# Scores of attentions A, B and C over all 128 rows with zeros for the other head; one visit of TensorE per attention slot; B's two maps combined before they are transposed

## The reference, cut to what matters

```
A: 8 query heads, 2 key heads, width 64, window |i-j| <= 128, a sink logit in the denominator
C: 3 patterns of 8 heads, width 64 (C0: window 64; C1, C2: among tokens of one residue mod 4)
D: 8 heads, width 96, all 512 keys
B (differential), 4 heads, two maps of width 64 each, all 512 keys, values of width 128:
    sc = einsum('bqmhd,bsmhd->bmhqs', q, k) * scale - slope[h] * |pos_q - pos_s|
    a  = softmax(sc, axis=-1)
    a  = a[:, 0] - lam[h] * a[:, 1]
    o  = einsum('bhqs,bshv->bqhv', a, v);   o = rms_norm(o, subln_g) * (1 - lam_init)
```

## Time and profile before

| | |
|---|---|
| time, median of 3 | 3000.47 us (3000.18 to 3017.97) |
| the profiled execution | 3004.72 us, its span 3002.9 us |
| PE busy | 2820.7 us, 94% of the span |
| PE weight load | 2267.0 us, 75% |
| DVE busy | 1566.0 us, 52% |
| ACT busy | 1179.0 us, 39% |
| chain that ended last | PE 81%, DVE 9%, ACT 4%, issue 4% |
| mean granted TensorE clock | 0.978 |
| DMA | 217.62 MB, mean 72 GB/s |

### The profile page before, as it was taken

The page is one execution under the profiler, slowest core; times in us unless marked ns, Lnnn a source line. Parts: engine busy times, 40 slices in busy tenths (PEclk is TensorE's granted clock), DMA queues, the critical chain, the costliest instruction groups (busy, mean ns, idle before and its releaser), DMA issues.

```text
span 3002.9 us, 44753 instructions
## 1 busy us (share of the span) xinstructions
PE 2820.7 (94%) x13358; PEld 2267.0 (75%) x13358; DVE 1566.0 (52%) x3238; ACT 1179.0 (39%) x2387; POOL 0.6 (0%) x5
## 2 busy tenths in 40 slices
PE   5999989989989998999979999898899899999998
PEld 4889978666667887888868898776666678788887
DVE  5454476444445445555644544764354454465655
ACT  4444444434433234332434444534444332342432
POOL 0000000000000000000000000000000000000000
PEclk9999999889999999999989999999999999999999
DMA  4212222001112332333332122220111123223332
GB/s 152 72 48 72 78 63 85 12 29 41 45 37 78 94 96 78 99 98 99 99 100 64 44 78 79 67 85 1 36 43 50 31 91 98 92 85 98 95 96 91
DMA packets 141819, 217.62 MB, mean 72 GB/s; under 512 B 14777, under 2 KB 69387, under 8 KB 141195
## 3 DMA queue, kind: packets, MB, share of 16 engines
q1 hardware_dynamic: 132521, 200.62, 21.4%
q10 hardware_dynamic: 9058, 14.06, 1.4%
HBM read 206.20 MB, written 8.45 MB: 71 GB/s over the span
## 4 chain that ended last, share of the span: by engine, by line
PE 81%; DVE 9%; ACT 4%; issue 4%; ACTq 1%; DMA 1%; DVEq 0%; SPq 0%
PE bank L452 21%; PE bank L454 20%; PE bank L453 20%; PE bank L665 7%; PE bank L655 6%; PE bank L503 5%; DVE s_work L1563 1%; DVE s_wl L1139 1%; ACT s_wh L776 1%; ACT s_work L1027 1%; DVE s_work L1294 1%; PE bank L539 1%; ACTq L874 1%; DMA s_raw<-in_w_in 0%; ACT s_work L1019 0%
## 5 line engine op out<-in xcount | busy, mean ns | idle before, releaser
L1139 DVE TENSOR_TENSOR s_wl<-s_raw,s_wh 128x1024 fp32r<-128x1024 f32 (+2 forms) x372 | 453.6, 1220 | 526.5 <-ACT s_wh L776 525.9
L776 ACT ACTIVATE s_wh<-s_raw 128x1024 fp32r<-128x1024 f32 (+2 forms) x372 | 392.2, 1055 | 625.1 <-PE bank L454 591.9
L452 PE MATMUL bank<-s_hTh,s_wh 128*128 128x512 f32 x1216 | 486.2, 400 | 4.5 <-DVE s_work L1231 4.5
L454 PE MATMUL bank<-s_hTh,s_wl 128*128 128x512 f32 x1216 | 476.9, 392 | 0.0
L453 PE MATMUL bank<-s_hTl,s_wh 128*128 128x512 f32 x1216 | 476.7, 392 | 0.0
L452 PE MATMUL bank<-s_wh,s_hTh 128*128 128x512 f32 (+1 forms) x1088 | 475.8, 437 | 0.0
L454 PE MATMUL bank<-s_wh,s_hTl 128*128 128x512 f32 (+1 forms) x1088 | 427.0, 392 | 0.0
L453 PE MATMUL bank<-s_wl,s_hTh 128*128 128x512 f32 (+1 forms) x1088 | 426.7, 392 | 0.0
L1019 ACT ACTIVATE s_work<-s_work,s_stat 128x128 f32<-128x128 f32 (+3 forms) x384 | 214.1, 558 | 369.5 <-DVE s_stat L1588 123.0
L1563 DVE COPY s_work<-bank 128x256 f32<-128x256 f32 (+1 forms) x288 | 105.2, 365 | 394.5 <-ACT s_work L1027 391.9
L503 PE MATMUL bank<-s_consts,s_work 128*128 128x128 f32 (+1 forms) x1560 | 250.0, 281 | 47.3 <-DVE s_gTl L1495 14.3
(11 more groups left out here) (166 smaller groups left out, 3199.6 us busy)
## 6 DMA issues: line engine op xcount, KB each, us to landing
s_raw<-in_w_in SPq DMA_DIRECT2D x168, 512.0 KB, 3.4
s_raw<-in_ffn_w_up SPq DMA_DIRECT2D x176, 256.0 KB, 2.9
s_raw<-in_ffn_w_down SPq DMA_DIRECT2D x44, 512.0 KB, 3.7
s_raw<-in_w_branch SPq DMA_DIRECT2D x32, 512.0 KB, 3.6
s_raw<-in_w_o SPq DMA_DIRECT2D x16, 512.0 KB, 3.6
x_keep<-s_work ACTq DMA_DIRECT2D x2, 2048.0 KB, 7.5
s_raw<-in_w_in SPq DMA_DIRECT2D x16, 256.0 KB, 2.9
s_work<-x_keep ACTq DMA_DIRECT2D x2, 2048.0 KB, 8.2
```

The source lines that it names most:

```text
L452: mm(out, stationary[0], moving[0], start=start, stop=False)
L454: return mm(out, stationary[1], moving[0], start=False, stop=stop)
L776: a(wh[:, k % 3, 0:n], raw[:, s, 0:n], ACT.Copy).then_inc(*hi_split.up(own))
L1139: v.tensor_tensor(wl[:, k % 3, 0:n], raw[:, k % 2, 0:n], wh[:, k % 3, 0:n].bitcast(F32), ALU.subtract).then_inc(*tile_split.up(own))
```

## The change

**Scores.** A new buffer `q_pad` (128 rows, 4 chunks, 2 halves, 128 queries) is set to zero once. ACT copies q of the current units into it: rows 0 to 63 into half 0, rows 64 to 127 into half 1 (stream `pads`, 8 pieces of two copies for each of C0, A and B, one copy for each unit of C1 and C2). The scores of A, B and C take a half of `q_pad` (128 rows, of which 64 are zero) as stationary operand and all 128 rows of k as moving one. PE waits for `q_padded`. D is as before.

**One visit.** In a slot PE now does transpositions of unit n-2, values of unit n-3 and scores of unit n one behind the other. ACT and DVE follow in that order. Tiles of `turns` that are due within 0.7 steps of a slot move to it (`in_visit`).

**B.** Its window ends at `START["gate1a"] - 4` instead of `START["gate0a"]`. DVE combines the two maps of a head, `p0 + (lam * sum0 / sum1) * p1`, into `mixed` (L1706 of the kernel after); that is transposed and multiplied once, and divided by the first sum at the end of a query tile. The norm of B's outputs starts at the window's end.

**Weights.** To make room a weight buffer is 1024 wide instead of 1152, so the two projections `dq0` and `dq1` take two tiles each (768 and 384 wide) instead of one; a layer has 94 tiles, and no longer a multiple of three, so the buffers' turn shifts at the layer's start. There two tiles are split by ACT ahead of `squares` and one by DVE ahead of `normalise`, the rest later.

```diff
-HALF = 384 * 3
+HALF = 512 * 2
-    D=(START["Aq"] + 14, START["Bq"], 32), A=(START["Bq"], START["gate3a"], 32), B=(START["gate3a"] + 1, START["gate0a"], 32),
+    D=(START["Aq"] + 14, START["Bq"], 32), A=(START["Bq"], START["gate3a"], 32), B=(START["gate3a"] + 1, START["gate1a"] - 4, 32),
...
                 for step, at, pace in slots(name):
...
-                    if step < n:
-                        yield at
...
-                    if 2 <= step < n + 2:
-                        yield at + pace / 3
-                        u = step - 2
+                    yield at
+                    if 2 <= step < n + 2:
+                        u = step - 2
+                        lo, hi, _mid = keys(u)
+                        pe.wait_ge(*p_ready.at(l, first + u + 1))
                         pe.wait_ge(*ta_act.at(l, n_att[0]))
                         pe.wait_ge(*ta_dve.at(l, n_att[0]))
                         n_att[0] += 1
+                        transposed(TA, [probs[:, u % 2, P * k:P * k + P] for k in range(lo, hi)], ta_ready, at=lo)
+                    if 3 <= step < n + 3:
+                        u = step - 3
                         pe.wait_ge(*ta_act.at(l, group[u]))
                         pe.wait_ge(*ta_dve.at(l, group[u]))
...
-                    if 1 <= step < n + 1:
-                        yield at + 2 * pace / 3
+                    if step < n:
...
+                        if name in PADS:
+                            pe.wait_ge(*q_padded.at(l, pads + pads_of(name, step)))
+                        pe.wait_ge(*s_biased.at(l, first + step))
+                        for out, st, mv in scores_of(step, S1):
+                            last = mm(out, st, mv, start=True, stop=True)
+                        last.then_inc(*s_ready.up())
...
-                        return [(out[:, P * lo:P * hi], q[head_rows(h), h // 2, P * t:P * t + P], k_of(h)[:, P * lo:P * hi])]
+                        return [(out[:, P * lo:P * hi], q_pad[:, h // 2, h % 2, :], k_of(h)[:, P * lo:P * hi])]
...
+                            a(q_pad[part, order(g), half, :], q[part, order(g), P * t:P * t + P], ACT.Copy).then_inc(*q_padded.up(own))
...
+                        v.scalar_tensor_tensor(mixed[:, u // 2 % 2, :], p1, share, p0, ALU.mult, ALU.add).then_inc(*b_mixed.up(own))
...
+            split_next()
+            split_next()
             squares(-8)
-            for _k in range(3):
-                split_next()
```

More of the change, by code:

```diff
@@ L169, in slots, with in_visit @@
     return [(step, begin + (end - begin) * step / (n + 4), (end - begin) / (n + 4)) for step in range(n + 4)]
+def in_visit(when):
+    for name in WINDOW:
+        for _step, at, _pace in slots(name):
+            if abs(at - when) <= 0.7:
+                return at - 0.01
+    return when
 def all_keys(u):
@@ L221, in _build @@
     krr = sb("krr", [P, TT, ROPE])
+    q_pad = sb("q_pad", [P, 4, 2, P])
     ident = consts[:, 0:P]
@@ L289, in _build @@
     ta_dve = signal("ta_dve", before=1)
+    q_padded = signal("q_padded")
     s_ready = signal("s_ready")
@@ new lines, in pads, with tiles_of, residues_of @@
+            def pads():
+                done = 0
+                def tiles_of(name, q, turns_done, order):
+                    nonlocal done
+                    first, n = done, WINDOW[name][2]
+                    done += n
+                    slot = slots(name)
+                    for piece in range(8):
+                        t, g = piece // 2, piece % 2
+                        yield slot[4 * piece - 4][1] + 0.8 * slot[0][2] if piece >= 2 else slot[0][1] - 0.5
+                        if piece == 0:
+                            act.wait_ge(*td_dve.at(l, turns_done))
+                        if piece >= 2:
+                            act.wait_ge(*s_ready.at(l, first + 4 * piece - 4))
+                        elif first:
+                            act.wait_ge(*s_ready.at(l, first))
+                        for half in range(2):
+                            part = slice(64 * half, 64 * half + 64)
+                            act.wait_ge(*own.done(l))
+                            a(q_pad[part, order(g), half, :], q[part, order(g), P * t:P * t + P], ACT.Copy).then_inc(*q_padded.up(own))
+                def residues_of(j, turns_done):
+                    nonlocal done
+                    first = done
+                    done += 8
+                    slot = slots(f"C{j}")
+                    for h in range(8):
+                        yield slot[h - 1][1] + 0.6 * slot[0][2] if h >= 2 else slot[0][1] - 0.5
+                        if h == 0:
+                            act.wait_ge(*td_dve.at(l, turns_done))
+                        act.wait_ge(*s_ready.at(l, first + h - 1 if h >= 2 else first))
+                        part = slice(64 * (h % 2), 64 * (h % 2) + 64)
+                        act.wait_ge(*own.done(l))
+                        a(q_pad[part, :, h % 2, :], CQ[j][part, h // 2, :].rearrange("p (r n) -> p r n", r=RES), ACT.Copy).then_inc(*q_padded.up(own))
+                by_pair, by_map = (lambda g: slice(2 * g, 2 * g + 2)), (lambda g: slice(g, 4, 2))
+                yield from tiles_of("C0", qT, 9, by_pair)
+                for j in (1, 2):
+                    yield from residues_of(j, 8 * j + 9)
+                done += WINDOW["D"][2]
+                yield from tiles_of("A", qA, 57, by_pair)
+                yield from tiles_of("B", qT, 65, by_map)
@@ new lines, in attention_b @@
+            def attention_b():
+                first, n = n_unit[0], WINDOW["B"][2]
+                n_unit[0] += n
+                for step, at, pace in slots("B"):
+                    if 3 <= step < n + 3 and step % 2 == 1:
+                        yield at + 0.05 * pace
+                        pair = (step - 3) // 2
+                        src = att_group()
+                        act.wait_ge(*o_ready.at(l, first + pair - 1))
+                        a(probsT[:, pair % 2, 0:2 * P], src[:, 0:2 * P], ACT.Copy).then_inc(*ta_act.up(own))
+                    if step < n:
+                        yield at + 0.35 * pace
+                        act.wait_ge(*s_biased.at(l, first + step + 1))
+                        if step >= 4:
+                            act.wait_ge(*b_mixed.at(l, step // 2 - 1))
+                        a(probs_b[step // 2 % 2][:, step % 2, :], scores[:, step % 2, :], ACT.Exp, scale=-1.0, bias=stat[:, 5, step:step + 1],
+                          accum_out=stat[:, 8, step:step + 1]).then_inc(*p_ready.up(own))
@@ L1073, in _ @@
                 direct(lam_in[:, n, :], io[name][L].rearrange("a h n -> a (h n)").broadcast_to([P, 256]))
-            together(dense(), turns(), attentions(), splits())
+            together(dense(), turns(), pads(), attentions(), splits())
         act.wait_ge(*params_in.at(DEPTH, 0))
@@ L1636, in attentions @@
                                      keys=near_keys, tile_at=4)
-                yield from attention("B", biased_b, out_b, 4)
+                yield from attention_b()
+            split_next()
             normalise()
-            for _k in range(3):
-                split_next()
             dve.wait_ge(*params_in.at(l, 0))
```

290 lines of the change are left out of this document (173 added, 117 removed).

## The result

The changed kernel takes 2899.43 us (median of 4 runs, 2893.43 to 2912.96), the one before on the same chip 3002.63 us (4 runs): ratio 0.965 [0.960, 0.970]. That is 103 us, not the 180 of the prediction, and 24 us above the top of its range. The profiled execution took 2912.96 us, 91.8 less than that of before.

A forecast was written before the change was run, and what follows sets the result against it. PE, busy 94% of the span, was taken to bound the kernel by its stream plus its holes. Terms 87 + 42 + 6 + 13 + 8 + 14 + 6 + 5 - 1 = 180 us, from 3000.5 to 2820 us; range 2765 to 2875.

The forecast's parts named there:

- Scores on 64 rows: Scores of A, B and C: 128 rows with zeros save 0.39 us for each of 224 units, 87 us.
- The rival that zeros don't help: Scores: the surcharge hangs on f32 scores after other work, not on rows; 93 us gained, 2907 us; chance 0.06.
- B's maps combined: B: 16 of 32 sets of transpositions and values a layer go, 1.32 us each, 42 us.
- Fewer visits: PE leaves dense work 179 times a layer instead of 228; 6 us, bounds 0 to 15.
- D's window: D, without dense work: period falls from 2.66 to 2.45 us over 62 periods, 13 us, bounds 0 and 27.
- Clock in D: D: PE would be busier, so a third of 24 us lost to low clock returns, 8 us.
- PE's waits: A, B and C: 14 of about 17 us of PE's waits for probabilities go.
- behind the DMA issues: Values' wait of 7.5 us behind ACT's DMA issues shrinks; 6 us for both layers.
- Start of a layer: Layer start: norm and parameters ready earlier with a split moved behind; net 5 us for both, bounds -5 and 8.
- `q_pad` 1: Added ACT copies and two more weight tiles a layer cost 1 us, at most 8 in all.
- the slower rival: PE waits at `q_padded` for late copies; at 3 us each of 80 points 3060 us; chance 0.03.
- waits stay or move: Visits: values and scores queue behind a late exponential, so only 87 + 42 is gained, 2871 us; chance 0.13.

The follow-up runs named there:

- td_b_spread_fill: Changed kernel with D's tile of heads in the other bank, B's window ended earlier, DMA issues spread, dummies in eight D slots: 2843.6 us, 0.945.
- d_old_order: Changed kernel with D alone in the old order of a slot (tile of heads, scores, values, transpositions): 2872.5 us, 0.955.
- fill_stall: Changed kernel with ten dummy matmuls behind each of D's tile transpositions, where PE waits 2.4 us: 2881.9 us, 0.959.
- td_fill: Changed kernel with D's tile of heads in the other transposition bank and six dummies ahead of transpositions in D's slots 2, 3, 10, 11, 12: 2872.9 us, 0.956.

## Why the prediction was wrong

- **Scores on 64 rows, 87 us: right.** 76 by stretches, 85 by the medians. The rival that zeros don't help is out. The Trainium skill, page "TensorEngine Tiling (Array Packing)", Key Properties, says that changing the tiling mode drains TensorE. The 65 us that the prediction worked out for that rule alone are as far from the stretches' 76 as its 87, and further from the medians' 85; the pair's own 0.10 us did go (1.12 to 1.02), which the rule does not cover. The upper bound of 95 was added up wrongly: 224 x 0.39 and 0.15 more for 32 units are 92.
- **B's maps combined, 42 us: right.** 20.2 + 19.6 with the issues out of the way.
- **Fewer visits, 6 us: within its bounds, rather too small.** Measured only in C2: there PE leaves dense work 13 times less often in a layer and kv is 2 us shorter, 0.15 us each, the prediction's upper bound. The values then waited for `O1` and gave more back in cq.
- **D's window, 13 us: wrong, the step that failed.** "The next one is on DVE and ACT ... 2.45 ... 62 periods" found the circle of a plain unit to 0.04 us. It then took this circle for every unit, although in the trace of before only 26 of the 62 distances between D's scores are 2.66 us. Eight of D's slots in both layers also transpose a tile of heads, and the change moves that from ahead of the scores to behind them, into a bank that the next transposition needs. On DVE and ACT it thereby comes behind the minimum and the exponential, and PE waits 2.35 us. The prediction had named this sign of being wrong, "a new long wait ahead of the visits' transpositions". At full clock this makes eight units 24.4 instead of 23.2 us. By 2.45 for each they should have taken 19.6, and even the circle alone, with the result of heads, gives 22.1. The first twelve units, too, run by other limits (tiles of k and of A's q are turned between them) and got 3 us longer, dummies included. The term is 0 at best (`td_b_spread_fill`, `d_old_order`).
- **Clock in D, 8 us: wrong sign.** "PE would be busier" did not hold at the tile visits. I priced a stall at its length. Here a stall of 2.4 to 2.8 us had 10 to 18 us at half clock behind it, where each unit costs 4.27 instead of 2.5; with the stall filled, the clock was back within 7 us of its fall. Half clock in the stretch went from 42 to 143 us. `fill_stall` puts the part of the clock that hangs on the stall at 9 to 16 us a layer.
- **PE's waits 14, behind the DMA issues 6: the waits went, their worth was less.** 50.9 us in L665 are gone, 7.5 became 2.2. But beyond rows, maps and DMA wait the stretches of C, A and B show 13 us, where waits and visits were put at 20, and cq and the part up to Aq took 12 more. That the issues' cover differs with the slots I had not seen: with both maps apart the same issues cost 10.1, with slots of 2.0 steps 8.0.
- **Start of a layer 5: right**, 3.6 and 2.5. **`q_pad` 1: 3 to 4**, and the slower rival is out.
- **Costed at nothing, and not nothing:** cq +7.2 (values of C2 at `O1`), gate2a to Aq +5.2, and B's norm ahead of br1a, 9 a layer. The last does not show in the sum of B's stretch; I take it that the waits and visits that went there pay for it, which was not measured.

The sum over rows, maps, start and issues held. The time lies between "waits stay or move" (2871) and "zero rows don't help" (2907). The former is right in that a wait moved, not in which: the tile's copies hold the next transposition, where it spoke of values and scores behind a late exponential. 0.13 was too little for it, and its price of 51 us was too small, since it left the clock out.

Not settled: what makes the clock fall at D's start and at the short waits for `O1`; why the old order of D lost 23 us to the clock in one layer of `d_old_order` and nothing in the other, with the same instructions; and how much of the 5.2 us between gate2a and Aq belongs to which of the moved transpositions.

## What to carry to other kernels

When an order is changed, follow the rare visits as well as the steady one: the one in eight that also serves another tile sets the worst stall. In a stretch with no dense work beside it, a stall of TensorE can cost more than its length, as the clock stays down behind it, so ask at each whether something can stand in it, dummies if need be. Work that one engine does in one piece, such as 16 DMA issues, can be hidden by slots of one length and not by shorter ones; split it before slots are made denser.

## What the runs showed of the hardware

- An f32 score on 64 of 128 rows, among matmuls on 128 rows, cost 0.34 us more than the same with 64 rows of zeros added (76 us for 224 units), and 0.1 of it lay between the two records of one matmul.
- Ten unused matmuls in each stall of 2.35 us shortened the phases at half clock from 14 to 24 us to 3.4 to 6.8 us. Six of them in eight slots kept the clock up (0.98 and 1.00 in D's window, where the changed kernel has 0.73 and 0.75, with the long stall itself gone too), but in `td_fill` the fall only came at a later wait.
- The clock fell behind waits of PE of 0.9 to 1.35 us in five of six tile visits (at 628.41 us, behind the 1.34 us that end at 628.22), before the longer stall had begun.
- The same instructions in two layers can differ by 23 us through the clock alone (126.9 and 149.6), so D must be judged at a named clock.
- 16 small DMA issues in one piece kept ACT 9.6 to 10.2 us, about 0.6 us each.
